# First attention: two heads' parts in pairs on the two halves of the array, and one activation table for the root mean square

## What is computed

```python
def first_block(x, ...):
    x = layer_norm(x, emb_ln_g, emb_ln_b)
    q, k, v, u = split(x @ w_in)                 # each 512 wide
    o = stick_breaking_attention(heads(q), heads(k), heads(v))   # 8 heads of 64
    o = o * rsqrt(mean(o * o, axis=-1) + 1e-6)   # per head and token
    o = o * attn_out_g
    pooled = multiscale_pool(u, w_pool, pool_scale)
    mixed = concatenate([o, pooled]) @ w_out
    ...                                          # layer norms, feed forward, embedding

def stick_breaking_attention(q, k, v):
    # z = q.k / sqrt(64), for s < t only
    # A[t,s] = sigmoid(z_ts) * prod over s<j<t of (1 - sigmoid(z_tj))
    # out[t] = sum over s of A[t,s] v[s]
```

## Time and profile before

| | |
|---|---|
| median of three runs | 4082.92 us (4072.54 to 4084.28) |
| the profiled execution's own time | 4080.43 us |
| its span, first to last instruction | 4078.7 us |
| mean granted clock of TensorE | 0.959 of full speed |
| TensorE matmul, busy | 3786.1 us, 93% |
| VectorE, busy | 2176.6 us, 53% |
| ScalarE, busy | 989.1 us, 24% |
| GpSimd, busy | 402.8 us, 10% |
| first scores of the first attention | at 108.6 us |
| first matmul of the next stage | at 485.4 us |

### The profile page before, as it was taken

One profiled execution on the slowest core, in us unless ns is written; L12 is line 12 of the kernel. 1 busy time (PEld: TensorE's weight loads), 2 busy tenths in 40 slices (PEclk: granted clock), 3 DMA queues, 4 the chain that ended last, 5 costly groups with the idle time before them and its releaser, 6 DMA issues. The chain is left out here.

```text
span 4078.7 us, 43456 instructions
## 1 busy us (share of the span) xinstructions
PE 3786.1 (93%) x17243; PEld 2987.8 (73%) x17243; DVE 2176.6 (53%) x2929; ACT 989.1 (24%) x1994; POOL 402.8 (10%) x172
## 2 busy tenths in 40 slices
PE   8999889999999969987879999996999999989998
PEld 6665577888887758766658888885777777767487
DVE  6555548655557565989564444446322223346394
ACT  1455430000003241134230000004012222232362
POOL 0112113223221001413000000000000000000000
PEclk9999799999999989999889999998999999999899
DMA  4100112232222111120111111122111212142122
GB/s 154 32 21 21 52 57 92 76 110 82 76 112 96 43 65 44 40 73 1 37 63 62 41 44 59 41 72 104 42 52 52 75 52 71 41 180 92 58 63 78
DMA packets 137387, 267.57 MB, mean 66 GB/s; under 512 B 11680, under 2 KB 42516, under 8 KB 137236
## 3 DMA queue, kind: packets, MB, share of 16 engines
q1 hardware_dynamic: 137236, 265.50, 18.3%
HBM read 220.39 MB, written 45.09 MB: 65 GB/s over the span
## 5 line engine op out<-in xcount | busy, mean ns | idle before, releaser
L130 PE MATMUL banks<-region_parts 128*128 128x512 f32 x3226 | 1287.6, 399 | 90.3 <-DVE weight_chunks_parts L124 64.8
L132 PE MATMUL banks<-region_parts,weight_chunks_parts 128*128 128x512 f32 x2112 | 828.3, 392 | 0.0
L130 PEld LDWEIGHTS banks<-region_parts 128*128 128x128 f32 x3226 | 612.2, 190 | 262.1 <-issue 77.4
L131 PE MATMUL banks<-weight_chunks_parts,region_parts 128*128 128x512 f32 x1984 | 779.2, 393 | 0.0
L131 PE MATMUL banks<-region_parts 128*128 128x512 f32 x1658 | 649.6, 392 | 0.0
L132 PE MATMUL banks<-region_parts 128*128 128x512 f32 x1568 | 616.1, 393 | 0.0
L132 PEld LDWEIGHTS banks<-region_parts,weight_chunks_parts 128*128 128x128 f32 x2112 | 399.7, 189 | 85.4
L131 PEld LDWEIGHTS banks<-weight_chunks_parts,region_parts 128*128 128x128 f32 x1984 | 377.5, 190 | 81.0 <-issue 4.4
L618 ACT ACTIVATE region<-constants 128x512 f32<-128x512 f32 x128 | 81.1, 634 | 1259.3 <-DVE constants L550 1259.3
L131 PEld LDWEIGHTS banks<-region_parts 128*128 128x128 f32 x1658 | 314.0, 189 | 65.2 <-issue 2.4
L132 PEld LDWEIGHTS banks<-region_parts 128*128 128x128 f32 x1568 | 297.6, 190 | 63.2
(11 more groups left out here) (390 smaller groups left out, 5030.3 us busy)
## 6 DMA issues: line engine op xcount, KB each, us to landing
weight_chunks<-in_w_in SPq DMA_DIRECT2D x19, 2048.0 KB, 8.2
weight_chunks<-in_w_up SPq DMA_DIRECT2D x16, 2048.0 KB, 8.7
weight_chunks<-in_w_down SPq DMA_DIRECT2D x16, 2048.0 KB, 7.8
extra<-in_w_ada SPq DMA_DIRECT2D x16, 1536.0 KB, 11.1
x_spill<-region SPq DMA_DIRECT2D x32, 512.0 KB, 10.7
weight_chunks<-in_w_out SPq DMA_DIRECT2D x8, 2048.0 KB, 8.4
region<-x_spill SPq DMA_DIRECT2D x32, 512.0 KB, 6.0
f_spill<-region SPq DMA_DIRECT2D x64, 256.0 KB, 2.0
```

What stands on the lines that cost most here:

```text
L130: pe.matmul(out, m.parts(lhs[0]), m.parts(rhs[0]), start=first, stop=False)
L131: pe.matmul(out, m.parts(lhs[0]), m.parts(rhs[1]), start=False, stop=False)
L132: return pe.matmul(out, m.parts(lhs[1]), m.parts(rhs[0]), start=False, stop=last)
```

## The change

It changes four things in `embed_attention_1`.

1. `parts` now alternates the two heads of a pair: the same tile and the same half of the keys for the even and then the odd head. Steps `2j` and `2j + 1` are thus two parts of equal width, on rows 0 to 63 and 64 to 127. In tiles with two parts, both upper parts come first, then both lower ones.
2. TensorE issues the scores of both parts at the even step, each after `z_free` has counted the sigmoids of all earlier pairs. The transposes of part `i - 2` now stand ahead of the side matmuls of the step, not behind them.
3. ScalarE does the sigmoids of both parts at the even step. VectorE does at the even step the weights of the last two parts and then the caps of the next two.
4. `rms` loads the table with both Ln and Exp by name before it waits for the sums.

```diff
--- before.py
+++ after.py
@@ -2832,7 +2832,7 @@
 
     groups = [(pair, half) for pair in range(N_HEADS // 2) for half in range(2)]
     units = [(gi, t, odd) for gi, (_, half) in enumerate(groups) for t in range(4 * half, 4 * half + 4) for odd in range(2)]
-    parts = [(n, c) for n, (gi, t, _) in enumerate(units) for c in range(t // 4, -1, -1)]
+    parts = [(n + odd, c) for n, (gi, t, _) in enumerate(units) if n % 2 == 0 for c in range(t // 4, -1, -1) for odd in range(2)]
     NP = len(parts)
     PP = NP // 4
     last_part = {}
@@ -2978,7 +2978,7 @@
                 if t == 0 and odd == 0:
                     pe.wait_ge(wt.bank_free, NBANK + (12, 18, 26, 34)[pair])
                 if i >= 2:
-                    pe.wait_ge(s.z_free, i - 1)
+                    pe.wait_ge(s.z_free, i // 2 * 2)
                 pe.matmul(m.bank[:, i % 2, 0:w], q[b:b + 64, pair, t * P:(t + 1) * P],
                           k[b:b + 64, pair, c * HALF:c * HALF + w], start=True, stop=True).then_inc(s.z_done, 1)
 
@@ -3023,15 +3023,17 @@
             pe.wait_ge(s.cols_ready, 1)
             pending = []
             for i in range(NP + 4):
+                if i < NP and i % 2 == 0:
+                    scores(i)
+                    scores(i + 1)
+                if 2 <= i < NP + 2:
+                    turn(i - 2)
                 if i < NP:
-                    scores(i)
                     if i in pooled_at:
                         pooled(*pooled_at[i])
                     if i in project_at:
                         c, g, j = project_at[i]
                         project(c, g, number[c, g], j)
-                if 2 <= i < NP + 2:
-                    turn(i - 2)
                 if i >= 4:
                     values(i - 4)
                     if pending and pending[0][0] <= i:
@@ -3106,6 +3108,7 @@
                 act.activation(mixT[:, pair, half * HALF:(half + 1) * HALF], m.bank[:, 6 + gi % 2, :], ACT.Copy).then_inc(s.out_taken, 1)
 
             def rms(gi):
+                act.preload_act_table_set(EXP_LN)
                 act.wait_ge(s.ss_done, gi + 1)
                 m.act_link(act, act.activation(sq, m.bank[:, 6 + gi % 2, :], ACT.Ln, bias=m.eps_col(RMS_EPS)))
                 act.activation(sq, sq, ACT.Exp, scale=-0.5).then_inc(s.rs_ready, 1)
@@ -3137,7 +3140,9 @@
             taken = done = 0
             for i in range(NP + 3):
                 if i < NP:
-                    sigmoids(i)
+                    if i % 2 == 0:
+                        sigmoids(i)
+                        sigmoids(i + 1)
                     if i in pooled_at:
                         pooled_out(*pooled_at[i])
                     if i in project_at and project_at[i][2] == 3:
@@ -3264,10 +3269,12 @@
             m.dve_link(dve, dve.tensor_tensor(m.c_act, m.c_act, m.cols("c", 0, 8), ALU.mult))
             mixes = 0
             for i in range(NP + 1):
-                if i:
+                if i and i % 2 == 0:
+                    weights(i - 2)
                     weights(i - 1)
-                if i < NP:
+                if i < NP and i % 2 == 0:
                     cap(i)
+                    cap(i + 1)
                 if i in split_at:
                     c, k0, k1 = split_at[i]
                     if k0 == 0:
```

## The result

| | before | after |
|---|---|---|
| median, same chip | 4083.49 us (4 runs, 4072.54 to 4084.28) | 4025.62 us (4 runs, 4022.96 to 4028.46) |
| profiled execution, own time | 4080.43 us | 4027.82 us |
| span | 4078.7 us | 4025.8 us |

The ratio is 0.9866 (95% interval 0.9853 to 0.988). The kernel is 58 us faster by the medians and 52.6 by the profiled executions; the 14 executions of the kernel before that ran beside e1 have a median of 4080.71 us, which would make it 55.

What follows compares the result with a forecast made beforehand. TensorE's matmuls bound the first attention's first three quarters, a loop over three engines the last. Terms: 7.2 + 11.5 - 2 + 4.8 + 1.3 + 12 = 34.8 us off 4082.9, so 4048 us, range 4030 to 4070.

Steps and rivals of the forecast that it cites:

- The passes of a pair: TensorE, first three quarters: score passes on different rows overlap, three slots instead of four, 11.5 us; upper bound 23.
- Rival 2: Paired scores on TensorE: the two halves overlap fully, a pair costs 1.05 us, 11.5 us more gain, 4037 us; chance 0.08.
- The fixed part: TensorE, first three quarters: adjacent scores pay the fixed 0.2 us once, 36 pairs, 7.2 us gained.
- The start: Start of the first attention: parts 4 and 6 start later, a loss of 2 us (0 to 4).
- The transposes ahead: TensorE's transposes moved ahead of the projection: costed at nothing, with about 1 to 3 us of slack.
- The bubbles: Quarters two and three: TensorE's 2.4 us waits at the projection for a bank both go, 4.8 us gained.
- The end: End of the stage: one bare table load between the last Ln and the last mix goes, 1.3 us gained.
- The last quarter: Last pair of heads: VectorE's idle shrinks by 7 (sigmoids under products), 4.8 (roots) and 1; taken as 12 us.
- the roots: Last quarter: VectorE's idle at the two roots falls from 5.6 and 6.6 us to 2.4 and 3.8, 4.8 less.
- Rival 3: The last quarter keeps its time, TensorE staying at the half clock; the 12 us go, 4060 us; chance 0.12.
- Rival 4: Ahead of every score pair: both scores wait for the last sigmoid, 65 us lost, 30 slower, 4113 us; chance 0.04.
- Rival 5: The table preload adds loads instead of removing them; 4.8 + 1.3 + about 3 us go, 4057 us; chance 0.03.

Runs made afterwards that it cites:

- e1: The changed kernel with both scores of a pair on rows 0 to 63 (even head's computed twice, odd head's left out): 4053.71 us, ratio 0.9935.
- e3: The changed kernel with the transposes back behind the side matmuls of the step: 4031.06 us, ratio 0.9877.
- e6: The kernel before the change with only the line that names the joint Ln and Exp table: 4075.91 us, ratio 0.9981.
- e2: The changed kernel without the preload of the joint Ln and Exp table: 4032.39 us, ratio 0.9881.
- e5: The changed kernel with the old order on ScalarE and VectorE, keeping TensorE's part and the table: 4064.55 us, ratio 0.9957.
- e9: The changed kernel with both heads' values issued at the even step, all of one head, then all of the other: 4012.88 us (one run).
- e7: The changed kernel with both heads' values issued at the even step, tile by tile in turn: 4001.52 us, ratio 0.9806.
- e8: The changed kernel with GpSimd's ten subtractions of the last quarter held until the last weights are done: 4030.64 us (one run).
- e4: The changed kernel with the second score of a pair issued at the odd step: 4079.74 us, ratio 0.9997.

## Why the prediction was too small

- **The passes of a pair: the step that failed.** I wrote "Three slots instead of four" and "I take 11.5, since the order of issue excludes 23 unless the engine reorders". B1 starts before A2 in all 48 pairs: a full pair costs 1.06 us (after) against 1.91 (e1), and the term is 22.4 us. So "Nothing is reordered at run time" in the description of the kernel does not hold for TensorE. Rival 2, given 0.08, was the true case, and by e1 its extra is 10.9 us. The row that speaks for it was not in the kernel before; both bounds were right, and the reason for the choice between them was an assumption about order within one queue. That passes on different rows run together at all was an assumption as well, in my 11.5 as in rival 2; the changed kernel shows it, with two starts within 0.01 us, for fp32 in two passes.
- **The fixed part, 7.2.** It held: 0.19 us a full pair (e1), and 7.9 us of matmul time by what is left in the sum below. What TensorE does in it, no run shows.
- **The start, -2.** It was less: TensorE's idle time in the first quarter rose from 0.6 to 1.4 us, where its loads wait for products (2.2 us) and once for sigmoids (1.4 us).
- **The transposes ahead, nothing.** 4.1 us (e3), of which 3.5 are matmul time. The slack of 1 to 3 us was enough: L2991 waits for a product for 0.8 us in the second and third quarters.
- **The bubbles, 4.8.** The term was read from a row of weight loads. The loads waited 4.8 us, and the matmuls less. Their own wait in these two quarters, in the kernel before, is

```profile
PE banks L130 <- ACT region L3069: 3.2, 2, 1.6
```

  and all their idle time there is 3.5 us, so no more could be won. In the changed kernel it is 0. Neither cause does it alone: with the table and the old order the loads' wait is 2.3 us (e6), with the new order and no table 1.5 (e2).
- **The end, 1.3.** As forecast (e6: 16.2 to 14.9).
- **The last quarter, 12.** It gave 15.2, in the bounds. Its parts by the experiments: 11.8 for the caps, sigmoids and weights in pairs (e5), where I had 7 + 1 and, in the 4.8 for the roots, what the loads do not explain (4.8 - 2 by 1.28 = 2.2); 3.3 for the table in the new order (e2) beside 0.1 alone in the old (e6); 2.6 for the overlap (e1), which I had not counted here. They overlap and need not add up. Rival 3 was wrong: the clock rose to 0.83.
- **Rival 4, the wait for both banks.** Off in the changed kernel, but the closest to being true: in e5 the first three quarters lose 28.2 us, 18.5 of them as idle time of the matmuls. I gave it 0.04 from slack worked out for the new order of all engines, which was right for that order only.
- **Rival 5.** Wrong by the table loads.

The 37.2 us of the first three quarters add up from the stretches. The matmuls' busy time fell by 34.5 us: 23.1 are the overlap (e1 against the changed kernel), 3.5 the transposes (e3 against it), and the 7.9 that are left are the fixed part, by difference. Their idle time fell by 2.7: 3.5 of it in the second and third quarters, less 0.8 more in the first. By length e1 gives 22.4 and not 23.1, since it stands idle for 0.7 us less in the first quarter.

So the forecast of 34.8 is short of the stage's 53.7 by 18.9 us: about 11 of them are the passes, 4 the transposes and 3 the last quarter. With 22.4 in the place of 11.5 alone it would have been 4037, inside the range.

Open: why the last quarter grows by 2.0 us with the values paired, though TensorE has less to do (the clock there is 0.69, below the 0.83 of the changed kernel, but in e9 the quarter is as long, 81.9 us, at 0.81; in e7 the values now wait 6.0 us for copies in three places, and VectorE is busy for 1.1 us more); why the table alone gives only 0.1 us in the last quarter; and how the 11.8 us divide between ScalarE and VectorE.

## What to carry to other kernels

Before assuming that work in TensorE's queue keeps to its order, look whether neighbours use different rows or columns of the array: here two 64-row scores cost what one did (1.06 us against 1.05), and so did two heads' values with 64 output partitions each, when they were interleaved instruction by instruction (0.86 us against 0.85); with six or eight loads of one head ahead of the other's, only part of it came (1.35 us with eight). Such a pairing must be carried through all engines of the loop: with TensorE's part and the table alone the stage kept 13.7 us of 53.7. Read what a wait costs from the matmuls' row and not only from the loads' (3.2 us against 4.8 here). Price side engines too: work of GpSimd that looked "hidden" stretched VectorE's by 12.7 us in the last quarter, the one stretch here where VectorE is the bound.

## What the runs showed of the hardware that I had not expected

- Two scores of two passes each, written A1, A2, B1, B2, start in pairs, the second matmul less than 0.01 us behind the first, and cost 1.06 us together instead of 1.91 on the same rows.
- Halves of the output columns overlap as well: sixteen 128x64 loads with their matmuls in 0.86 us when interleaved, 1.35 us when one head's eight stand before the other's. Up to three loads were passed by the other half's first one, in 34 pairs (e9).
- 26.6 us of GpSimd's busy time in the last quarter cost VectorE 12.7 us of its own (e8).
- The order of the same matmuls within a step changed their busy time by 1.3 us in 78 (e3), at the same clock, 1.00.
- Waits of the weight loads cost the matmuls less than they show: 4.8 us of the loads were 3.2 of the matmuls (the bubbles, kernel before), and 17.8 were 0.8 (e4's transposes).
